# A feed-forward that runs two chunks ahead, its inner values turned by DMA alone, and half of x turned by DMA in three stages

## The reference, cut to what matters

```python
def rms_norm(x, g):
    x32 = x.astype(jnp.float32)
    y = x32 * lax.rsqrt(jnp.mean(x32 * x32, axis=-1, keepdims=True) + EPS)
    return y.astype(x.dtype) * g

def swiglu(x, w_gate, w_up, w_down):
    return (jax.nn.silu(x @ w_gate) * (x @ w_up)) @ w_down
```

## Time and profile before

| | |
|---|---|
| median of 3 runs | 1210.16 us (1208.95 to 1210.77) |
| span of the profiled execution | 1207.7 us |
| PE busy | 1199.7 us (99%) |
| DVE busy | 773.3 us (64%) |
| ACT busy | 691.9 us (57%) |
| POOL busy | 68.3 us (6%) |
| the four feed-forwards | about 5 to 186, 369 to 549, 731 to 912, 1023 to 1204 us |
| HBM read | 219.78 MB |

### The profile page before, as it was taken

One profiled execution on the slowest core, in us unless ns is written; L12 is line 12 of the kernel. 1 busy time (PEld: TensorE's weight loads), 2 busy tenths in 40 slices (PEclk: granted clock), 3 DMA queues, 4 the chain that ended last, 5 costly groups with the idle time before them and its releaser, 6 DMA issues.

```text
span 1207.7 us, 17122 instructions
## 1 busy us (share of the span) xinstructions
PE 1199.7 (99%) x5662; PEld 989.7 (82%) x5662; DVE 773.3 (64%) x1089; ACT 691.9 (57%) x1012; POOL 68.3 (6%) x119
## 2 busy tenths in 40 slices
PE   9999999999999999999999999999999999999998
PEld 7888888877788888888888788888888887888887
DVE  6665555688685556567678766665556667655554
ACT  6555555676655555557666576655555546655543
POOL 0420000000000000000220110000000000000000
PEclk9999999999999999999999999999999999999999
DMA  9977754554465998745654517986655554776771
GB/s 333 245 226 223 216 178 154 167 175 140 157 220 166 244 245 257 217 155 160 201 168 164 174 66 232 252 230 198 200 155 167 164 168 145 213 221 201 219 226 44
DMA packets 208385, 232.01 MB, mean 192 GB/s; under 512 B 56080, under 2 KB 148368, under 8 KB 208336
## 3 DMA queue, kind: packets, MB, share of 16 engines
q1 hardware_dynamic: 163792, 214.61, 57.1%
q10 hardware_dynamic: 42752, 11.02, 5.0%
q0 software_dynamic: 1792, 5.75, 2.0%
HBM read 219.78 MB, written 1.05 MB: 183 GB/s over the span
## 4 chain that ended last, share of the span: by engine, by line
PE 96%; DVE 1%; DMA 1%; ACT 1%; issue 0%; ACTq 0%
PE bank L1971 30%; PE bank L1973 30%; PE bank L1972 30%; PE bank L2030 2%; PE bank L2198 1%; DMA sb_probs<-sb_probs 1%; PE bank L2214 1%; PE bank L2185 1%; PE bank L2183 0%; DMA sb_gates<-h_xT 0%; ACT sb_probs L1237 0%; PE bank L2060 0%; DVE sb_wl L1320 0%; PE bank L2502 0%; DVE sb_rmax L1866 0%
## 5 line engine op out<-in xcount | busy, mean ns | idle before, releaser
L1971 PE MATMUL bank<-sb_wh,sb_aTh 128*128 128x512 f32 (+1 forms) x1124 | 435.6, 388 | 0.0
L1973 PE MATMUL bank<-sb_wh,sb_aTl 128*128 128x512 f32 (+1 forms) x1124 | 431.0, 383 | 0.0
L1972 PE MATMUL bank<-sb_wl,sb_aTh 128*128 128x512 f32 (+1 forms) x1124 | 430.7, 383 | 0.0
L1320 DVE TENSOR_TENSOR sb_wl<-sb_raw,sb_wh 128x1024 fp32r<-128x1024 f32 x269 | 325.4, 1221 | 102.4 <-ACT sb_wh L733 98.1
L733 ACT ACTIVATE sb_wh<-sb_raw 128x1024 fp32r<-128x1024 f32 (+1 forms) x275 | 285.7, 1048 | 117.5 <-PE bank L1973 43.8
L1973 PEld LDWEIGHTS bank<-sb_wh,sb_aTl 128*128 128x128 f32 x1124 | 211.2, 188 | 42.1
L1971 PEld LDWEIGHTS bank<-sb_wh,sb_aTh 128*128 128x128 f32 x1124 | 211.3, 188 | 40.9 <-DVE sb_wl L1320 0.4
L1972 PEld LDWEIGHTS bank<-sb_wl,sb_aTh 128*128 128x128 f32 x1124 | 211.4, 188 | 39.9
L1320 DVE TENSOR_TENSOR sb_wl<-sb_z,sb_wh 128x1024 fp32r<-128x1024 f32 x132 | 158.8, 1222 | 37.0 <-ACT sb_wh L733 36.9
L733 ACT ACTIVATE sb_wh<-sb_z 128x1024 fp32r<-128x1024 f32 x132 | 137.2, 1057 | 58.7 <-PE bank L1973 40.6
L1971 PE MATMUL bank<-sb_wh,sb_hTh 128*128 128x512 f32 x320 | 125.0, 391 | 0.4 <-DVE sb_hTl L1402 0.4
(11 more groups left out here) (218 smaller groups left out, 918.4 us busy)
## 6 DMA issues: line engine op xcount, KB each, us to landing
sb_raw<-w_in SPq DMA_DIRECT2D x80, 256.0 KB, 3.0
sb_z<-ffn_w_down SPq DMA_DIRECT2D x64, 256.0 KB, 4.7
sb_z<-w_down SPq DMA_DIRECT2D x64, 256.0 KB, 3.7
sb_raw<-w_gate SPq DMA_DIRECT2D x54, 256.0 KB, 3.5
sb_raw<-w_up SPq DMA_DIRECT2D x54, 256.0 KB, 4.2
sb_raw<-ffn_w_gate SPq DMA_DIRECT2D x51, 256.0 KB, 3.7
sb_raw<-ffn_w_up SPq DMA_DIRECT2D x51, 256.0 KB, 4.5
sb_raw<-e_w_in SPq DMA_DIRECT2D x40, 256.0 KB, 3.1
```

The lines of the kernel that those rows point to most:

```text
L1320: dve.tensor_tensor(wl[:, u % NSPLIT, :], raws[SLOT[u]], wh[:, u % NSPLIT, :].bitcast(F32), ALU.subtract).then_inc(low_done, 1)
L1971: pe.matmul(dst, lh, w_hi, start=start, stop=False)
L1972: pe.matmul(dst, lh, w_lo, start=False, stop=False)
L1973: return pe.matmul(dst, ll, w_hi, start=False, stop=stop)
```

## The change

In all four feed-forwards PE works two chunks ahead: gate and up of chunk c + 2, then down of chunk c. Chunks 0 to 10 all go through planes, DMA transpose and join; `transpose_hidden` and `ht_step` are gone. Chunk 2 uses banks 6 and 7. The last three downs follow one another without a gate and up between them; chunk 9 and chunk 10 get their halves in `aTh[:, 4:8]`, `aTl[:, 4:8]`.

In ffn1, ffn2 and ffn3 the second half of x (k = 4 to 7) is also turned by DMA: `x_planes` (ACT, two copies of 1024 values of 16 bits), `x_turn` (ACT's queue, 2048 columns), `x_join` (DVE, two copies), then `xt_high_turned` and `xt_low_turned` from the joined values. The `xt_half(norm, 1)` of these stages is gone. The first twelve units of these stages are in the order TURNED_FRONT, as pairs of chunk and i: five units that need only the first half of x, then seven of the rest.

The loads follow the new order of the units. The diff, cut to its core:

```diff
+TURNED_X = [(2, 1), (5, 1), (8, 1)]
+XT_GROUPS = [(norm, g) for norm in range(1, 9) for g in range(4) if (norm, g // 2) not in TURNED_X]
+TURNED_FRONT = [(0, 0), (0, 1), (1, 0), (1, 1), (2, 0), (0, 2), (0, 3), (2, 1), (1, 2), (1, 3), (2, 2), (2, 3)]
...
-                load_gate_up(u + 4 + i, f, i, c + 1, c)
+                load_gate_up(u + 8 + i, f, i, c + 2, c)
             for k in range(2):
-                load_down(u + 8 + k, f, 2 * c + k, c)
+                load_down(u + 12 + k, f, 2 * c + k, c)
         if f == 0:
             load_front()
         else:
-            for i in range(4):
-                load_gate_up(u + i, f, i, 0)
+            for n, (chunk, i) in enumerate(TURNED_FRONT):
+                load_gate_up(u + n, f, i, chunk)
+        if f == 0:
             load_pass(0)
-        with sp.Fori(1, NFC - 1, 1) as c:
+        else:
+            for k in range(2):
+                load_down(u + 12 + k, f, k)
+        with sp.Fori(1, NFC - 2, 1) as c:
             load_pass(c)
-        for k in range(2):
-            load_down(u + 64 + k, f, 2 * (NFC - 1) + k)
+        for k in range(4):
+            load_down(u + 62 + k, f, 2 * (NFC - 2) + k)
...
+    def x_planes(norm, half):
+        act.wait_ge(x_ready, 4 * (norm - 1) + 2 * half + 2)
+        dst = qk_slots[half].bitcast(U16).rearrange("p (h t c) -> p h t c", h=2, t=NT)
+        src = x[:, :, 512 * half:512 * half + 512].bitcast(U16).rearrange("p t (c h) -> p h t c", h=2)
+        for h in range(2):
+            ins = copy(dst[:, h], src[:, h])
+        ins.then_inc(x_planed, 1)
+    def x_turn(norm, half):
+        act.wait_ge(x_planed, TURNED_X.index((norm, half)) + 1)
+        act.dma_start_transpose(qk_slots[2 + half].bitcast(U16).rearrange("p (b r) -> p b r", r=P),
+                                qk_slots[half].bitcast(U16)).then_inc(x_turned, 16)
+    def xt_high_turned(norm, half):
+        col = NORM_FILL[norm][1]
+        act.wait_ge(x_joined, TURNED_X.index((norm, half)) + 1)
+        for j in range(4):
+            k = 4 * half + j
+            copy(aTh[:, k, :], qkT[:, half, j, :], vecs[:, col + k:col + k + 1]).then_inc(a_high, 1)
...
+        def hidden(c, v, c6=0):
+            split(v, c6)
+            planes_step(c)
+            act.wait_ge(planes_done, NFC * f + c + 1)
+            split(v + 1, c6)
             turn_hidden()
+        def body(c, bank_=0):
+            v = u + 8
+            split(v, c)
+            split(v + 1, c)
+            turned_step(c, hTh[:, :, :])
+            split(v + 2, c)
+            split(v + 3, c)
+            act.wait_ge(units_used, v + 4 + 6 * c)
+            silu_step(c + 2, bank_)
+            hidden(c + 2, v + 4, c)
+        def turn_now(c):
+            planes_step(c)
+            act.wait_ge(planes_done, NFC * f + c + 1)
+            turn_hidden()
         if f == 0:
+            splits(u, 2)
...
+            rstd_known(norm)
+            act.wait_ge(units_used, u + 5)
+            silu_step(0, FFN_FIRST_BANK[f])
+            hidden(0, u + 3)
+            splits(u + 5, 3)
+            act.wait_ge(units_used, u + 8)
+            silu_step(1)
+            hidden(1, u + 8)
+            split(u + 10)
+            turned_step(0, hTh[:, :, :])
+            split(u + 11)
+            act.wait_ge(units_used, u + 12)
+            silu_step(2, 6)
+            hidden(2, u + 12)
+        else:
+            xt_high(norm, 0)
+            if f > 1:
+                splits(u - 2, 2)
+            x_planes(norm, 1)
+            split(u)
+            x_turn(norm, 1)
+            token_ssq(norm, x)
+            load_tables(SILU_SET)
+            splits(u + 1, 3)
+            xt_high_turned(norm, 1)
+            rstd_known(norm)
+            splits(u + 4, 4)
+            act.wait_ge(units_used, u + 7)
+            silu_step(0, FFN_FIRST_BANK[f])
+            split(u + 8)
+            turn_now(0)
+            splits(u + 9, 2)
+            act.wait_ge(units_used, u + 10)
+            silu_step(1)
+            turned_step(0, hTh[:, :, :])
+            split(u + 11)
+            turn_now(1)
+            split(u + 12)
+            if f == 2:
+                km_split(1, 4)
+            act.wait_ge(units_used, u + 12)
+            silu_step(2, 6)
+            if f == 2:
+                km_turn(1)
+            planes_step(2)
+            act.wait_ge(planes_done, NFC * f + 3)
+            split(u + 13)
+            turn_hidden()
+        with act.Fori(1, NFC - 3, 1) as c:
+            body(c)
+        body(NFC - 3)
+        turned_step(NFC - 2, aTh[:, 4:6, :])
+        splits(u + 62, 2)
+        turned_step(NFC - 1, aTh[:, 6:8, :])
...
+    def x_join(norm, half):
+        n = TURNED_X.index((norm, half)) + 1
+        dve.wait_ge(x_turned, 16 * n)
+        dst = qk_slots[half].bitcast(U16).rearrange("p (k t r h) -> p h k t r", k=4, t=NT, h=2)
+        src = qk_slots[2 + half].bitcast(U16).rearrange("p (h t k r) -> p h k t r", h=2, t=NT, k=4)
+        for h in range(2):
+            ins = dve.tensor_copy(dst[:, h], src[:, h])
+        ins.then_inc(x_joined, 1)
+    def xt_low_turned(norm, half):
+        fill, col = NORM_FILL[norm]
+        for j in range(4):
+            k = 4 * half + j
+            dve.wait_ge(a_high, 8 * fill + k + 1)
+            dve.scalar_tensor_tensor(aTl[:, k, :], qkT[:, half, j, :], vecs[:, col + k:col + k + 1],
+                                     aTh[:, k, :].bitcast(F32), ALU.mult, ALU.subtract).then_inc(a_low, 1)
...
-            if norm is not None:
+            if norm is not None and (norm, half) not in TURNED_X:
...
         def join_step(c):
+            if not (isinstance(c, int) and c == 0):
+                dve.wait_ge(ht_low, NFC * f + c)
+            dve.wait_ge(planes_turned, 16 * NFC * f + 16 + 16 * c)
...
+        def turned_step(c, low, high):
             dve.wait_ge(ht_high, NFC * f + c + 1)
+            dve.tensor_tensor(low, hT, high.bitcast(F32), ALU.subtract).then_inc(ht_low, 1)
+        def body(c, bank_=0):
+            v = u + 8
+            split(v, c)
+            split(v + 1, c)
+            turned_step(c, hTl[:, :, :], hTh[:, :, :])
+            split(v + 2, c)
+            join_step(c + 1)
+            split(v + 3, c)
+            mul_step(c + 2, bank_)
+            split(v + 4, c)
+            split(v + 5, c)
         if f == 0:
+            splits(u, 3)
+            mul_step(0, FFN_FIRST_BANK[f])
+            splits(u + 3, 5)
+            join_step(0)
+            mul_step(1)
+            splits(u + 8, 3)
+            turned_step(0, hTl[:, :, :], hTh[:, :, :])
+            split(u + 11)
+            join_step(1)
+            mul_step(2, 6)
+            splits(u + 12, 2)
+        else:
+            splits(u, 4)
+            x_join(norm, 1)
+            xt_low_turned(norm, 1)
+            splits(u + 4, 4)
+            mul_step(0, FFN_FIRST_BANK[f])
+            splits(u + 8, 3)
+            join_step(0)
+            mul_step(1)
+            turned_step(0, hTl[:, :, :], hTh[:, :, :])
+            splits(u + 11, 2)
+            join_step(1)
+            mul_step(2, 6)
+            split(u + 13)
+        with dve.Fori(1, NFC - 3, 1) as c:
+            body(c)
+        body(NFC - 3)
+        turned_step(NFC - 2, aTl[:, 4:6, :], aTh[:, 4:6, :])
+        split(u + 62)
+        join_step(NFC - 1)
+        split(u + 63)
+        turned_step(NFC - 1, aTl[:, 6:8, :], aTh[:, 6:8, :])
...
+        def gate_up(v, bank_, c=0, begun=0):
             for i in range(begun, 4):
+                square(v + i, 2 * i, aTh, aTl, bank_, i == 0, i == 3, c)
+        def down_unit(v, k, high, low, c=0, start=False):
+            pe.wait_ge(low_done, v + 1 + 6 * c)
             for n in range(2):
                 for t in range(NT):
+                    ins = down(v, k, n, t, start, False, high, low)
             ins.then_inc(units_used, 1)
+        def body(c, bank_=0, start=False):
+            if bank_ == 0:
+                pe.wait_ge(h_ready, 2 * NFC * f + 4 + 2 * c)
+            gate_up(u + 8, bank_, c)
+            pe.wait_ge(ht_low, NFC * f + 1 + c)
+            for k in range(2):
+                down_unit(u + 12 + k, k, hTh, hTl, c, start and k == 0)
         if f == 0:
...
+            gate_up(u + 4, 0, begun=1)
...
         else:
+            fill = 8 * NORM_FILL[norm][0]
+            for n, (c, i) in enumerate(TURNED_FRONT):
+                second = None
+                if (c, i) == (0, 0):
+                    pe.wait_ge(a_low, fill + 1)
+                    second = lambda: pe.wait_ge(a_low, fill + 2)
+                elif c == 0:
+                    pe.wait_ge(a_low, fill + 2 * i + 2)
+                elif (c, i) == (1, 0):
+                    pe.wait_ge(x_ready, 4 * norm)
+                square(u + n, 2 * i, aTh, aTl, (FFN_FIRST_BANK[f], 0, 6)[c], i == 0, i == 3, halfway=second)
+            pe.wait_ge(ht_low, NFC * f + 1)
             for k in range(2):
+                down_unit(u + 12 + k, k, hTh, hTl, 0, k == 0)
+        if f == 0:
+            body(0, 6, True)
```

(38 more changed lines are left out.)

95 lines of the change are left out of this document (9 added, 86 removed).

## The result

The changed kernel takes 1229.0 us (median of 5 runs, 1227.7 to 1231.5) beside 1210.3 for the kernel before, now also of 5 runs; the ratio is 1.016, 95% interval 1.0147 to 1.0172. The forecast was 1228, 1216 to 1237. The profiled execution has a span of 1227.2 us, before 1207.7: 19.5 us more.

A forecast was written before the change was run, and what follows sets the result against it. PE was taken as the bound, busy 1199.7 of 1207.7 us. From 1210.2, less 6.8 removed, plus 11.1 for x's waits, 3.2 for tails and 10.5 for first turns, came 1228.2, forecast as 1228 us, range 1216 to 1237.

The forecast's parts named there:

- waits for x: PE idles ahead of the sixth unit in ffn1 to ffn3, 3.7 us each, 11.1 us in all.
- tail: PE waits 0.8 us ahead of the down of chunk 9 in all four feed-forwards, 3.2 us in all.
- first turns: PE waits behind the first down for mul_step(2), after two successive transposes of chunks 0 and 1; 10.5 us, range 2 to 19.
- signs of being wrong: ACT copying k=4 earlier than 12.9 us, chunk 0 and 1 transposes landing under 5 us, or the granted clock falling.
- Removed, 6.8 us: Time off PE: hidden-value transposes 3.6 us, transposes of x 2.7 us, and ffn2's wait ahead of its first down 0.5 us.
- so 3 x 3.7: ffn1's wait for x carried over to ffn2 and ffn3 as equally long, 11.1 us together.
- landed long before, even at 6.9 us: In ffn1's chain, x's transpose lands well before the join's turn on DVE, so its length doesn't count.
- The allowances of 5.2 and 4.9 us: How long the transposes of chunk 0 and chunk 1 may take before each further us costs PE one.
- rival 4: Waits of 3.7 us and more drop PE's clock to half, 1.6 us each, four make 6.5: 1235 us; chance 0.08.
- Rival 1: Transposes of chunks 0 and 1 land as in the loop, so first turns cost nothing: 1217.7 us; chance 0.22.
- Rival 3: A transpose's issue doesn't hold ACT, so x's wait is about 1.5 us and the tail's gone: 1207.9; chance 0.06.
- The rule against the path's price: DMA transposes are as fast as other DMAs, so first turns would stay below 4.9 us and cost nothing.

The follow-up runs named there:

- e_best_xpe: Changed kernel with x's second half turned by PE again, plus reordered tail, nearer wait in PE's first loop pass and ffn0's chunk 0 first; 1207.4 us, ratio 0.9972.
- e_sp_issue: Changed kernel with x's transpose issued on SP's queue, not ACT's; in ffn2 and ffn3 the tenth unit's load waits for its landing; 1221.8 us, ratio 1.0093.
- e_order: Changed kernel with ACT's two sums of squares and table load moved behind the copies from the joined values in ffn1 to ffn3; 1238.5 us, ratio 1.022.
- e_loads: Changed kernel with SP holding the tenth unit's load and those after it until x's transpose has landed, in ffn2 and ffn3; 1228.7 us, ratio 1.0144.
- e_tail: Changed kernel with chunk 9's copy ahead of ACT's last split and its rest ahead of DVE's last rest, in every feed-forward; 1227.0 us, ratio 1.0131.
- e_both: Changed kernel with the edits of both e_order and e_loads; 1231.3 us, ratio 1.0165.
- e_sp_join: e_sp_issue with DVE's join and rests of x put ahead of the weight rests of u+6 and u+7; 1223.5 us, ratio 1.0111.
- e_best: e_sp_join with reordered tail, nearer wait in PE's first loop pass, and ffn0's chunk 0 copy and rest ahead of chunk 1's planes; 1217.7 us, ratio 1.0056.

## Why the prediction was right, point by point

The forecast of 1228 came within 1 us, and that it came so near is luck. The terms were off in both directions: waits for x, tail and first turns were 11.1 + 3.2 + 10.5 = 24.8 us and measured 14.3 + 2.4 + 3.6 = 20.3, the first 3.2 us short, the last 6.9 too long; the clock, put at nothing, took 3.7, and 1.2 came up in a place that nobody had looked at. The kinds of cost were named rightly. Of the prediction's own signs of being wrong two came true: the transposes of chunks 0 and 1 landed in under 5 us in ffn2 and ffn3 (4.0 to 4.8), and the granted clock fell.

**Removed, 6.8 us.** The count is right (5606 instructions). The size wasn't measured by itself; e_best_xpe, which removes 3.6 + 0.5 = 4.1 of it, is 3.1 below the kernel before, with 0.6 to 0.8 us each left at chunk 10 of ffn1 and at the unchanged place between ffn0 and ffn1 that had no idle in the trace before.

**The waits for x, 11.1 us; 14.3 measured.** For ffn1 the chain holds row by row: planes 2.0, issue 1.9, sums and table to the next split 380.41 - 376.77 = 3.64, join 1.35 as taken; 3.5 us against 3.7. The step that failed is "so 3 x 3.7", which carries ffn1's 1.90 us of issue to ffn2 and ffn3: there it took 3.4 and 4.0, which makes 1.5 + 2.1 us, while the rest of each chain was 0.2 us shorter than taken. e_sp_issue confirms it: with the issue off ACT's queue all three waits are 2.4 us. The sentence that the transpose "landed long before, even at 6.9 us" failed too, at 11.4 and 12.4 us, but cost 0.2 us at most; it only kept e_order from paying. Those transposes move 512 KB, and the row that the landing was priced by was one of 256 KB. In ffn1 two loads were issued in the 4 us behind the transpose, in ffn2 and ffn3 four, and e_loads, which held these back, showed them to be what makes the landing long. What makes the issue long stays open: e_loads didn't shorten it. In ffn2 and ffn3 of every run two loads had been issued 0.9 and 0.5 us ahead of the transpose, which e_loads left there, and in ffn1 none in the 4.5 us ahead; but on SP's queue in e_sp_issue the issue took 3.5 us in ffn1 as well, with none there.

**The tail, 3.2 us; 2.4 measured**, 0.59 in each, inside the 0.5 to 1.0 given; e_tail confirmed the place.

**The first turns, 10.5 us; 3.6 measured.** ffn0 0.9 (0.5 said, 0 to 2), ffn1 2.7 (6.4 said, 1.5 to 10), ffn2 and ffn3 nothing (1.8 each said). The mechanism stands: the waits come at 412.18 behind join and `mul_step(2)`, as told, and in e_order, e_both, e_sp_join and e_best, where chunk 0's transpose took 8.7 to 10.8 us, ahead of the first down, with 1.4 to 5.0 us. The allowances of 5.2 and 4.9 us hold as well: with ffn1's landings of 7.8 and 5.6 us they give 2.6 + 0.7 = 3.3. What failed is taking the old stages' landings as given: 6.9 and 5.0 for ffn2 and ffn3, 4.0 to 4.8 measured. For ffn2 even that isn't what the old trace had: it took 8.7 and 7.8 us there, so by its own rule the prediction would have added 6.4 us in place of 1.8 and come to 1233. The landing is not a property of the stage. It follows the loads queued just ahead of the issue and behind it (7 in the 5 us ahead and the last one 0.7 us ahead in e_both's ffn2, 2 and 2.6 us in the changed kernel's), and where x is turned by DMA the waits for x, which stand ahead, change just that. The two terms were added as if they were independent; when e_order took the first away in ffn1 and cut it a little in the others, the third grew to 9.6 us in these stages, 13 with the half clock behind it.

**The clock (rival 4, 0.08), 0 in the sum; 3.7 measured.** It fell behind two of the three waits for x. Its price of 1.6 us a fall was about right (2.2 and 1.5 here, where matmuls of 512 columns began 0.43 us apart; 1.4 to 2.9 in the other runs). The Trainium skill, "TensorE: Matmul & The Clock Gate", Part 1, has an idle array go back to half clock; the runs agree that it happens in mid-kernel, and show that the length of a wait alone doesn't say when: behind 3.5 us in ffn1 it stayed up (granted 1.00 in the 3 us behind), behind 3.5 us in e_loads' ffn1 it fell (0.50, 1.7 us lost), and of three waits of 2.4 us in e_sp_issue two let it fall.

**Rival 1 (free first turns, 1217.7)** was right on the turns of ffn2 and ffn3 and wrong on the total, as the waits for x and the clock were larger. **Rival 3 (the issue doesn't hold ACT)** is out: moving the issue to SP saved 7.3 us. **The rule against the path's price**, that transposes by DMA are as fast as other DMAs ("Advanced Engine Details and Errata", X-Bar Transpose (TRN2), of the Trainium skill): a quiet 256 KB transpose landed in 3.0 to 4.9 us, a weight load of 256 KB in 3.0 to 4.2 by the medians of the profile, so in a quiet queue the runs agree. In a burst both are slow, the transpose more so: x's transpose of ffn3 took 12.4 us (512 KB), the four loads issued beside it 7.1 to 10.8, and chunk 0's in e_both's ffn2 took 10.4 us, the four loads issued nearest to it 4.5 to 9.6. What failed is the conclusion from the rule, that a transpose would then land in time in ffn1.

**Not foreseen at all**: the 1.2 us in the unchanged stage between ffn0 and ffn1. An idle of 0.4 to 1.7 us ahead of the same transposes stood in every variant, and none in the kernel before; its cause wasn't tried and stays open; the profile shows nothing that PE waited for.

Also open: whether x's transfer, SP's hold, or the later splits of the eighth to eleventh unit put chunk 0's transpose so close behind the loads in e_sp_join. That wasn't tried apart.

## What to carry to other kernels

When a transfer joins a path that the busiest engine waits for, price it by what is queued in the few microseconds before and behind its issue, not by a mean of its kind, and give a range that goes to the worst landing seen; then ask what each wait that you add or remove does to the spacing of the loads behind it, because a stall upstream may be what makes the next transfer cheap. Where a sum comes out right, look at its terms before trusting it: here errors of 3 to 7 us cancelled. Count the cost of the issue on its own queue, don't carry it from one stage to another (here 1.9 and 4.0 us), and put a transpose that shares a queue with critical work on an engine that would only wait. Take a change of two parts apart before judging it: here one part gave 3 us after three small reorderings, and the other cost 16.

## What the hardware showed beyond this

The issue of one and the same transpose (512 KB) held ACT's queue 1.9 to 2.0 us in ffn1 and 3.3 to 4.1 us in ffn2 and ffn3, in every run that issued it there, whether the weight loads behind it were held or not, and PE's wait was its length plus 1.6 us in ten of the twelve stages of the four kernels that keep the change's order. Its landing went from 5.1 us in ffn1 to 11.4 and 12.4 in ffn2 and ffn3, and back to 5.3 and 6.7 there when the four weight loads issued in the 3 us behind it were held, and the loads beside it in ffn3 landed after 7.1 to 10.8 us, where those issued in ffn1 at 377 took 3.8 to 4.1. PE's clock fell behind waits as short as 2.0 us (e_loads, ffn0: granted 0.50 from 42.3 to 45.3 us) and stayed up behind one of 3.5 (the changed kernel, ffn1: 1.00 from 387.8 to 390.8).
